# Nine pairs of row buffers in place of eight for the last part of a gather ring

## The reference

```python
def mla_attend(q_lat, q_rope, ckv, krope, q_pos, k_pos):
    s = einsum('bqhc,bkc->bhqk', q_lat, ckv) + einsum('bqhr,bkr->bhqk', q_rope, krope)
    ...
    return einsum('bhqk,bkc->bqhc', softmax(s), ckv)

# sample: the keys are the cached pages and the 8 new positions of the row
ckv_all = concatenate([cache_ckv[l][page_table].reshape(db, past, KV_LORA), ckv_s], axis=1)

def peer_ffn(h, w_q, sub_keys, u_tab, v_tab):          # per token
    sc = einsum('thpd,hpnd->thpn', q, sub_keys)         # 8 heads, 2 halves, 128 keys
    s1, i1 = top_k(sc[:, :, 0], 16); s2, i2 = top_k(sc[:, :, 1], 16)
    ...                                                 # best 16 of the 256 sums
    e = i1[...] * 128 + i2[...]
    act = gelu(einsum('thkd,td->thk', u_tab[e], h))
    return einsum('thk,thkd->td', gate * act, v_tab[e])
```

## Time and profile before

| | |
|---|---|
| median of 3 runs | 3383.99 us (3381.88 to 3387.01) |
| the profiled execution | 3373.47 us, its span 3371.7 us |
| TensorE busy | 2965.6 us, 88% |
| VectorE busy | 2250.1 us, 67% |
| ScalarE busy | 1570.0 us, 47% |
| GpSimd busy | 1283.0 us, 38% |
| moved | 1298.60 MB, mean 385 GB/s |
| granted TensorE clock, mean | 0.954 |

### The profile page before, as it was taken

The page is one execution under the profiler, slowest core; times in us unless marked ns, Lnnn a source line. Parts: engine busy times, 40 slices in busy tenths (PEclk is TensorE's granted clock), DMA queues, the critical chain, the costliest instruction groups (busy, mean ns, idle before and its releaser), DMA issues.

```text
span 3371.7 us, 32678 instructions
## 1 busy us (share of the span) xinstructions
PE 2965.6 (88%) x9646; PEld 1528.1 (45%) x9646; DVE 2250.1 (67%) x5353; ACT 1570.0 (47%) x4252; POOL 1283.0 (38%) x1097
## 2 busy tenths in 40 slices
PE   7988899988989898989998888988897988898877
PEld 6754555543445444544444333443353434453322
DVE  1269737785578648884789568866777485873854
ACT  2137334555456344643455445644564354532443
POOL 0023323443344434443444444443434333443532
PEclk8988999989999999999999999999999998989999
DMA  4279999999999999999999999999999998999998
GB/s 175 91 298 358 393 391 397 395 414 420 421 407 396 422 422 418 400 398 413 417 410 422 421 422 421 415 422 422 413 357 406 422 373 311 380 377 380 420 422 346
DMA packets 238361, 1298.60 MB, mean 385 GB/s; under 512 B 45748, under 2 KB 70228, under 8 KB 95462
## 3 DMA queue, kind: packets, MB, share of 16 engines
q0 software_dynamic: 156672, 1140.92, 82.7%
q1 hardware_dynamic: 81510, 155.59, 12.4%
HBM read 1279.41 MB, written 16.44 MB: 384 GB/s over the span
## 4 chain that ended last, share of the span: by engine, by line
PE 45%; DMA 26%; DVE 21%; ACT 4%; issue 2%; SPq 1%; POOL 0%; DVEq 0%; ACTq 0%
PE PS L1080 21%; DMA R<-in_t_uv,idx 17%; DVE R L1729 8%; PE PS L763 8%; DMA R<-in_t_uv,idxS 4%; DMA wring<-in_w_out 3%; PE PS L1002 2%; PE PS L729 2%; PE PS L1029 2%; PE PS L844 2%; PE PS L843 2%; DVE SC L1695 2%; DVE SC L1692 2%; DVE xb L1740 2%; PE PS L825 1%
## 5 line engine op out<-in xcount | busy, mean ns | idle before, releaser
L1080 PE MATMUL PS<-R,diag 128*128 128x512 f32 x3776 | 1826.3, 622 | 229.4 <-ACT diag L1361 194.4
L694 POOL DMA_INDIRECT R<-in_t_uv,idx x1024 | 1218.7, 1190 | 1966.0 <-PE PS L1080 1367.4
L1729 DVE CUSTOM_DVE_ANT_0 R<-R,hb 128x1024 f32<-128x1024 f32 x1088 | 1318.4, 1222 | 751.4 <-DMA R<-in_t_uv,idx 668.9
L1080 PEld LDWEIGHTS PS<-R,diag 128*128 128x128 f32 x3776 | 699.3, 196 | 1133.0 <-issue 649.7
L1352 ACT ACTIVATE acts<-dots 128x1 f32<-128x1 f32 x1088 | 218.9, 201 | 1147.7 <-DVE dots L1729 1141.2
L1361 ACT ACTIVATE diag<-ident,wv 128x128 f32<-128x128 f32 x880 | 355.0, 403 | 102.8 <-PE PS L1080 75.2
L763 PE MATMUL PS<-R 128*128 128x256 f32 (+1 forms) x1280 | 294.8, 386 | 31.0 <-ACT stg L1123 16.4
L1354 ACT ACTIVATE wv<-gate,acts 128x1 f32<-128x1 f32 x1024 | 304.1, 297 | 33.4
L763 PEld LDWEIGHTS PS<-R 128*128 128x128 f32 x1280 | 244.5, 198 | 97.3 <-issue 65.8
L1740 DVE SCALAR_TENSOR_TENSOR xb<-R,wv,xb 128x1024 f32<-128x1024 f32 x144 | 184.7, 1282 | 3.3 <-ACT wv L1354 3.3
L1002 PE MATMUL PS<-wring,T 128*128 128x512 f32 x256 | 128.1, 628 | 30.8 <-DMA wring<-in_w_out 30.8
(11 more groups left out here) (243 smaller groups left out, 2375.2 us busy)
## 6 DMA issues: line engine op xcount, KB each, us to landing
wring<-in_w_out SPq DMA_DIRECT2D x64, 512.0 KB
wring<-in_w_query SPq DMA_DIRECT2D x64, 512.0 KB
R<-in_t_win SPq DMA_DIRECT2D x27, 1024.0 KB, 18.4
R<-in_t_uv,idx POOLq DMA_INDIRECT x1024
pr<-prd SPq DMA_DIRECT2D x8, 976.0 KB
prd<-stg SPq DMA_DIRECT2D x54, 128.0 KB
xb<-in_x_prompt SPq DMA_DIRECT2D x8, 512.0 KB, 3.6
R<-in_w_out SPq DMA_DIRECT2D x8, 512.0 KB, 5.4
```

Of the source, the lines that this page charges most:

```text
L694: e.indirect_dma_start(dst, None, table, bass.IndirectOffsetOnAxis(ap=index, axis=0)).then_inc(S[s], c.count(name, s, 16))
L1080: m = mm(bank(n), diag[:, NTH[s] % DR, :], pair(s)[:, D + 512 * n:D + 512 * n + 512], start=begins, stop=s == last_slot(t), skip_group_che ...
L1729: e.tensor_tensor_reduce(u, u, hb[:, tile_of(g) % 2, :], 1.0, 0.0, ALU.mult, ALU.add, dots[:, g % NW:g % NW + 1]).then_inc(dve_done, c.cou ...
```

## The change

The number of pairs from slot 776 to the end becomes nine. Pair 8 (`R[:, 16:18]`) stays in the ring, since the sample gets only the five buffers from `SAUX` = 18 on. Two buffers are saved by laying `kcT` (with `kdb`) and `krcT` into columns 0 to 1023 of `ckvT` and `krg`; these two grow to 1088 columns, and the sample's own new latents and keys go to columns 1024 to 1087. The room for that comes from `fval`, which now is the same memory as `ival`. `ldc` waits for the last slots before 776 that used pairs 9 and 10.

```diff
+SAUX = NR - 5
...
         if s == WIDE[1]:
-            free = deque(i for i in free if i < RN)
+            free = deque(i for i in free if 2 * i < SAUX)
...
-        ckvT = sb("ckvT", [P, NKEY])
-        krg = sb("krg", [P, NKEY])
+        ckvT = sb("ckvT", [P, SEQ + NSMP])
+        krg = sb("krg", [P, SEQ + NSMP])
...
-        fval = sb("fval", [P, 2 * H, TOPK])
...
+        fval = ival[:].bitcast(F32)
...
-        sst = R[:, AUX:AUX + 2, :].rearrange("p a (b c e) -> p (a b) c e", b=4, c=4)
-        cachev = [R[:, AUX + 2, :], R[:, AUX + 3, :]]
-        kcT = R[:, AUX + 4, :]
-        kdb = R[:, AUX + 4, :]
-        krcT = R[0:ROPE, AUX + 5, :]
-        krc = [R[:, AUX + 6, 0:256], R[:, AUX + 6, 256:512]]
-        latS = R[:, AUX + 6, 512:1024]
+        sst = R[:, SAUX:SAUX + 2, :].rearrange("p a (b c e) -> p (a b) c e", b=4, c=4)
+        cachev = [R[:, SAUX + 2, :], R[:, SAUX + 3, :]]
+        kcT = ckvT[:, 0:SEQ]
+        kdb = ckvT[:, 0:SEQ]
+        krcT = krg[0:ROPE, 0:SEQ]
+        krc = [R[:, SAUX + 4, 0:256], R[:, SAUX + 4, 256:512]]
+        latS = R[:, SAUX + 4, 512:1024]
...
-                wide = [s for s in range(NSLOT) if home(s) >= RN]
+                wide = [s for s in range(NSLOT) if s < WIDE[1] and 2 * home(s) + 1 >= SAUX]
...
-                    mm(at, qn, ckvT[:, DEC_T * b:DEC_T * b + DEC_T], start=True, stop=False)
-                    mm(at, qr, krT[:, DEC_T * b:DEC_T * b + DEC_T], start=False, stop=True).then_inc(
+                    mm(at, qn, ckvT[:, SEQ + DEC_T * b:SEQ + DEC_T * b + DEC_T], start=True, stop=False)
+                    mm(at, qr, krT[:, SEQ + DEC_T * b:SEQ + DEC_T * b + DEC_T], start=False, stop=True).then_inc(
...
-                    frm, dst = slice(0, NSMP), slice(0, NSMP)
+                    frm, dst = slice(0, NSMP), slice(SEQ, SEQ + NSMP)
```

More of the change, by code:

```diff
@@ L1675, in top @@
                 settle()
-                ts(pair(fval[:])[:, :, 0, :], pair(fval[:])[:, :, 0, :], 128.0, None, ALU.mult).then_inc(dve_done, c.count())
+                ts(pair(fval)[:, :, 0, :], pair(fval)[:, :, 0, :], 128.0, None, ALU.mult).then_inc(dve_done, c.count())
                 yield from p.to(6)
@@ L1680, in top @@
                 settle()
-                pair_sums(pair(fval[:]), cnde)
+                pair_sums(pair(fval), cnde)
                 yield from top16(heads, lambda l: cnd[:, l, :], best, bpos, 8)
```

## The result

The kernel after took 3391.22 us in the median, the one before 3382.46 in the same session: a ratio of 1.0036, 95% interval 1.0026 to 1.0047. The ratios and intervals in this document are estimates from the single runs of both kernels and not quotients of the two medians, from which they lie up to 0.0015 apart (the quotient here is 1.0026). One of the twenty runs of the kernel after was a slow one of 5847.29 us and is left out of the ratio. The change made the kernel slower, by 9 to 16 us; the forecast was 3377.5 and its range ended at 3388. The profiled execution took 3393.22 us, against 3373.47 for that of before. Lines of the kernel after are one higher than those of before.

A forecast was written before the change was run, and what follows sets the result against it. Expert gathers filling the transfer engines were taken as the bound, standing still at times for want of a free buffer. The terms, 2.9 + 0 + 1.1 + 2.5 - 0 = 6.5 us, took 3384.0 to 3377.5 us; range 3366 to 3388.

The forecast's parts named there:

- The other edits move no instruction and add none: Moved page keys, state-load waits and in-place index casts: taken as 0 in the sum, at most 0.9 and 4.2 us lost.
- The rule for one pair: Each consumer-paced stretch gives at most min(its standstill, 2.49 us), if a stretch paced by the transfers follows.
- the sum of 6.5 us: Total saving of the terms, 2.9 + 0 + 1.1 + 2.5 - 0; bounds 1.0 to 11.1 us.
- Term 1: Attention of the last prompt tile, 2444 to 2550 us: standstill 3.4 us, saving 2.9 (2.5 to 3.4).
- Term 2: Sample's attention, 2740 to 2975 us: some 20 us standstill, saving taken as 0 (2.5 lost to 2.7 gained).
- Term 3: Sample's retention and output projection, 2975 to 3100 us: saving 1.1 us, between 0 and 2.5.
- Term 4: Last pause, 3100 to 3118 us: standstill nearly closes, saving 2.5 us (1.9 to 2.5) that reaches the end whole.
- One gather more ahead of each load: Slower rival: loads on SyncE's queue stand behind issued gathers, each awaited load losing 2.49 us; 3400 us; chance 0.10.
- Every pause refilled: Rival: each pause gives its standstill up to 2.49 us, 14.8 in all, so 3369 us; chance 0.17 including more.
- weights and pages set the pace: Rival: an early gather is spent at the next load wait; saving 0 to 2.5 us, 3382 to 3384; chance 0.25.
- The signs that were to tell the rivals apart: Share of 2765 to 2845 rising; last pause remaining; TensorE's page and weight waits growing by 2.5 us each.
- the ceiling for all the pauses behind slot 776: Share 0.98 against a full 1.01 over 911 us: some 27 us of standstill, the most the change can save.

The follow-up runs named there:

- before_w128: Kernel before with a 128-byte tensor moved from ahead of the weight buffers to behind them, so these begin at remainder 128; 3390.52 us, 1.0022.
- before_shift: Kernel before with the row buffers moved 128 bytes lower, to the remainder of the kernel after (32); 3387.23 us, 1.0012.
- eight_moved: Kernel after with eight pairs to the end, row buffers at the same addresses as in the kernel after; 3392.23 us, 1.0037.
- eight_pad640: Kernel after with eight pairs and 640 unused bytes ahead of the row buffers, putting these back at their old place; 3389.02 us, 1.0016.
- nine_again: The kernel after timed once more, unchanged; 3391.22 us, 1.0038.
- nine_pad640: Kernel after with 640 unused bytes ahead of the row buffers, putting these back at their old place; 3381.70 us, 1.0006.
- the wide ones: Kernel after with each page loaded as 16 rows of 4 KB and of 1 KB: with eight pairs 3394.90 us, 1.0055; with nine 3391.23, 1.0045.
- eight_same: Kernel after with eight pairs and 128 unused bytes behind the rotary keys, giving every tensor but those keys its old remainder; 3376.28 us, 0.9996.
- nine_same: Kernel after with 128 unused bytes behind the rotary keys, giving every tensor but those keys its old remainder; 3373.48 us, 0.9978.
- before_align: Kernel before with the row buffers at remainder 0: 96 unused bytes ahead of them, sample indices moved behind; 3356.22 us, 0.9939.
- eight_pad480: Kernel after with eight pairs and 480 unused bytes ahead of the row buffers (remainder 0); 3359.15 us, 0.9939.
- nine_pad480: Kernel after with 480 unused bytes ahead of the row buffers (remainder 0); 3352.39 us, 0.9899.
- nine_480_again: Kernel after with 480 unused bytes ahead of the row buffers (remainder 0), timed again in a later session; 3358.82 us, 0.9935.
- nine_pad224: Kernel after with 224 unused bytes ahead of the row buffers, which then begin 256 bytes past a multiple of 512; 3351.27 us, 0.9916.
- nine_w512: Kernel after with the row buffers and the three weight buffers all at multiples of 512 bytes; 3354.66 us, 0.9926.

## Why the prediction was wrong, point by point

**The step that failed** is "The other edits move no instruction and add none", with the zero that stands for it in the sum. The sentence is true, and it priced the edits as if instructions were all that an edit can move. Two of them change the size of a tensor, and so the address of all that is declared behind it, the landing places of 1.1 GB of gathers and of the weights among it. The measured parts: the weights' address alone 0.0022 (before_w128), the rows' alone 0.0012 (before_shift, not clear of zero), together 0.0034, and 0.0037 with both and eight pairs (eight_moved). By the trace the rows' part is 8 ns x 1088 = 8.7 us, or 0.0026, and eight_moved lies 0.0021 over eight_pad640, nine_again 0.0032 over nine_pad640. That both addresses cost something is shown; how the 0.0037 divides between them is known only roughly.

**The rule for one pair and the sum of 6.5 us.** The sign was right, the size somewhat too large. Nine against eight pairs at the same addresses, by the medians: -1.0 us (nine_again), -3.7 (the wide ones), -7.3 (640 bytes), -2.8 (same), in the mean 3.7 us less; no single one of these is certain by itself. nine_same, which is the change without the moved addresses, stands 8.2 us below its session's before, or 0.0022 with an interval that holds the 6.5.

**The terms.** They fared worse than their sum. I take the four profiles with eight pairs (before, eight_moved, eight_pad640, eight_same) and the four with nine at the same addresses (after, nine_again, nine_pad640, nine_same), and count slots by the starts of their dot products; means in us, and the single values in their order:

| slots | holds | eight | nine | gain | forecast |
|---|---|---|---|---|---|
| 776 to 876 | Term 1 | 292.9 (293.9, 294.7, 291.8, 291.0) | 292.7 (294.0, 293.3, 292.0, 291.4) | 0.2 | 2.9 |
| 876 to 939 | Term 2 | 213.9 (208.0, 216.3, 219.9, 211.2) | 217.0 (219.0, 221.0, 209.9, 218.1) | -3.1 | 0 |
| 939 to 990 | Term 3 | 155.3 (156.8, 157.5, 153.7, 153.2) | 150.8 (152.2, 150.1, 149.3, 151.5) | 4.5 | 1.1 |
| 990 to 1087 | Term 4 | 252.4 (251.6, 252.8, 252.6, 252.4) | 253.0 (252.7, 253.5, 252.4, 253.3) | -0.6 | 2.5 |

Term 1: the shares rose by 0.06 x 12 and 0.05 x 20, 1.7 us of the 2.9, and slot 781's gather is 2.3 us ahead relative to slot 776; at slot 876 nothing of it is left. Term 4, which I held for the surest, gave nothing: slot 991 comes 3 us earlier, but then slot 992, the gather that waits for slot 983 with nine pairs, takes over the whole wait. The share rose from 0.87 to 0.93, yet more gathers had been fetched ahead and the pause had moved by one, not shrunk. Term 3 is the real gain, and the only stretch in which the four values on either side do not overlap: here, in the retention and the output projection, I read that the consumers catch up more than once and find an early gather each time, but no run tested that, and part of it may be Term 2's loss coming back. The four gains add up to 1.0 us, where the timed runs have 3.7; with single profiles that far apart neither contradicts the other.

In the kernels with aligned rows it comes out otherwise. Between the two with eight pairs (before_align, eight_pad480) and the four with nine (nine_pad480, nine_480_again, nine_pad224, nine_w512) the gains are 5.0, -6.3, 7.4 and -0.4 us, in all 5.7, near the forecast sum; here Term 1 and Term 3 both stand clear of the single values' scatter (292.6 and 291.5 us against 286.5 to 287.4, and 159.9 and 159.8 against 151.7 to 153.2). So Term 1's gain is there in these kernels and not in the others, and in both sets slots 876 to 939, which Term 2 put at nothing, take longer with nine pairs (3.1 and 6.3 us). Why, no run shows.

Term 2 is the least settled. The waits for pages grew by 11.8 us in the kernel after, but they differ almost as much between kernels with the same number of pairs: over eight kernels with eight pairs and the old page rows these waits are 9.6 to 17.7 us, mean 13.7, and over nine with nine pairs 9.7 to 21.4, mean 16.3. Row 6's load took 17.8 us before, and 31 to 32 in after, nine_again, nine_same and eight_pad640 alike. What the waits cost in the end is little: taking away 20 us of them changed no median beyond its scatter. My reading, which no run tests by itself: the transfers are busy meanwhile (1.01 from 2890 to 2923), and what they bring then is not waited for later.

**The rivals.** "One gather more ahead of each load", the slower one, has the right sign and, as the cause of the loss, the wrong mechanism. Its price in waits may be there (2.6 us between the two means), but with wide page rows the waits go and the time stays, and with eight pairs the time is as long. Landing at 3391 beside its 3392 is chance. While gathers are queued, a load's small packets and a gather's large ones go through one for one, whether eight or nine pairs are in use: 483 of 512 or 128 bytes beside 483 of 8 KB from 2797 to 2807 us before, 1155 beside 1151 from 2810 to 2834 after. That is some 128 of a load's 2048 per gather of 128; where the gathers pause they go far faster, 958 in the 2 us from 2808 before. The Trainium skill ("DMA: Bandwidth & Descriptors", section "Queues, rings and completion order") has each engine take the queue rows in turn, and the counts agree with it. "Every pause refilled" and "weights and pages set the pace" would both have been faster or even. The signs that were to tell the rivals apart did not: the share of 2765 to 2845 rose a little (0.57 to 0.59, 0.69 to 0.73), which was to speak for the first, the last pause remained, for the second, and the waits for pages grew, as for the third, while that for weights fell from 5.14 to 3.63 us, against it. Only the experiments told them apart.

The forecast carried no bound for the address, as for a thing with no instruction. The trace of before did hold a hint that went unread: a queue that is full at 1.01 and moves 420 GB/s is a rate, and a rate may depend on where it is going.

## What to carry to other kernels

When an edit changes the size or the order of tensors, work out the start address of each large DMA destination before and after, by 256 bytes, and price a change of remainder as a change of the transfer rate; here 0.1 to 0.6%, as much as the edit's purpose or more. In a kernel whose transfer share is at its full value, try those start addresses first: before_align won 23.8 us by the medians (21 by the ratio) with 96 bytes of padding and one small tensor moved, most of what the prediction set as the ceiling for all the pauses behind slot 776 (27). And to judge a change that moves addresses, build the variant that pads them back (nine_same); without it nine pairs would have been thrown away for a fault they don't have.

## What the runs showed of the hardware that had not been expected

- Gathers of 1 MB (128 partitions of 8 KB), one behind the other, landed every 2.444 to 2.445 us with their destination at a multiple of 256 bytes, 2.484 to 2.485 at a remainder of 128 or 160, and 2.492 at 32. That the remainder counts is measured; why it does, and why 32 costs a little more than 160, no run shows. Each buffer is a whole number of 256 bytes, so all had the same remainder. Other remainders were not run.
- The weights' loads (4 KB a partition) beside the gathers cost 0.0022 of the kernel when their buffers went from remainder 0 to 128 with the rows at 160. With the rows aligned no such cost was seen: 0.9926 with the weights aligned, 0.9935 without, intervals overlapping. How a slower 4 KB packet (166.5 ns mean in before_w128, 164.9 before: 1.6 x 21904 / 16 = 2.2 us) makes some 7 us is open: a part may be that the stretch of gathers beside them moves less (420 GB/s before, 419 in before_w128), which no run separates.
- A page load of 2048 small packets took 14 to 36 us in the sample's attention, one of 256 large packets 18 to 23 (30 once): steadier, hardly sooner on the whole.
